# Small spaces between the buffers of the split weight panels and in front of y

## What is computed

```
# first block, per layer
h = x @ w_in                       # split into the parts of three attentions
ya = moba(a_q, a_k, a_v) * silu(a_z)      # 8 heads of 64, causal, ALiBi
yb = mla(rmsnorm(b_cq) @ w_uq, rmsnorm(b_ckv) @ w_ukv) * silu(b_z)
yc = rmsnorm(diff_attention(c_q, c_k, c_v)) * silu(c_z)
g = sigmoid(x @ w_m + b_m)
out = (ga * (ya @ w_a) + gb * (yb @ w_b) + gc * (yc @ w_c)) @ w_o
r = ALPHA * x + out
x = layernorm(r + sigmoid(r @ w_pg) * (p_i @ w_p))
# second block, per layer (modulation rows from cond @ ada_w)
h = h + gate * swiglu(modulate(rmsnorm(h)), ffn1)          # width 2816
h = h + gate * (concat(retention, stick_breaking, mamba2) @ w_out)
h = h + gate * swiglu(modulate(rmsnorm(h)), ffn2)
```

## Time and profile before

| | |
|---|---|
| median of three runs | 2030.14 us |
| runs | 2029.02, 2034.85, 2030.14 us |
| profiled execution | 2016.13 us |
| its span, first to last instruction | 2014.8 us |
| mean granted TensorE clock | 0.972 |
| TensorE busy | 1897.4 us, 94% |
| VectorE, ScalarE busy | 1311.2 us, 942.6 us |

### The profile page before, as it was taken

How to read it: one execution, slowest core, us unless ns; L and a number is a source line. 1 busy time by engine, 2 the same in 40 slices (tenths; PEclk the granted TensorE clock), 3 DMA queues, 4 the chain that set the end, 5 groups by cost and what they waited for, 6 DMA issues and landing times.

```text
span 2014.8 us, 33982 instructions
## 1 busy us (share of the span) xinstructions
PE 1897.4 (94%) x15008; PEld 1815.9 (90%) x15008; DVE 1311.2 (65%) x1850; ACT 942.6 (47%) x1266; POOL 43.8 (2%) x48
## 2 busy tenths in 40 slices
PE   7998998899899987999999889999999999999998
PEld 7987888898788886999899789999999999889998
DVE  5666677665776676666766866666666675765554
ACT  5564454445545454444455334334444455434443
POOL 0000100000010000000000000000000000000000
PEclk9999999999999998999989999999999999999999
DMA  7444356464353552766455334665566555334551
GB/s 300 178 190 157 147 204 217 163 260 178 129 223 132 208 225 118 287 251 250 168 220 200 146 127 188 251 251 230 209 244 248 199 192 209 116 120 151 197 188 63
DMA packets 59284, 389.70 MB, mean 193 GB/s; under 512 B 6656, under 2 KB 9472, under 8 KB 15232
## 3 DMA queue, kind: packets, MB, share of 16 engines
q1 hardware_dynamic: 59136, 387.52, 50.9%
HBM read 386.45 MB, written 1.05 MB: 192 GB/s over the span
## 4 chain that ended last, share of the span: by engine, by line
PE 69%; DVE 19%; ACT 10%; issue 1%; DMA 0%; POOL 0%; SPq 0%; DVEq 0%; ACTq 0%
PE bank L698 21%; PE bank L700 21%; PE bank L699 21%; DVE weights_split L847 6%; ACT weights_split L841 4%; PE bank L762 2%; ACT map L1282 1%; DVE xbc L2145 1%; DVE map_stat L1470 1%; ACT map L1288 1%; DVE weights L827 1%; PE bank L897 1%; DVE map L1464 1%; DVE hidden L2157 1%; DVE u L2163 1%
## 5 line engine op out<-in xcount | busy, mean ns | idle before, releaser
L847 DVE TENSOR_TENSOR weights_split<-weights,weights_split 128x2048 fp32r<-128x2048 f32 (+2 forms) x306 | 655.3, 2142 | 421.0 <-ACT weights_split L841 420.4
L698 PE MATMUL bank<-u,weights_split 128*128 128x256 f32 x2048 | 589.0, 288 | 17.8 <-DVE u L2163 10.1
L841 ACT CAST weights_split<-weights 128x2048 fp32r<-128x2048 f32 (+2 forms) x306 | 543.3, 1776 | 126.8 <-PE bank L700 100.8
L699 PE MATMUL bank<-u,weights_split 128*128 128x256 f32 x2048 | 577.7, 282 | 0.0
L700 PE MATMUL bank<-u,weights_split 128*128 128x256 f32 x2048 | 577.0, 282 | 0.0
L698 PEld LDWEIGHTS bank<-u,weights_split 128*128 128x128 f32 x2048 | 390.9, 191 | 25.2 <-DVE u L2163 13.4
L700 PEld LDWEIGHTS bank<-u,weights_split 128*128 128x128 f32 x2048 | 392.3, 192 | 0.0
L699 PEld LDWEIGHTS bank<-u,weights_split 128*128 128x128 f32 x2048 | 391.7, 191 | 0.5 <-issue 0.5
L698 PE MATMUL bank<-y,weights_split 128*128 128x256 f32 (+1 forms) x1168 | 331.7, 284 | 4.2 <-ACT b_k L867 4.2
L699 PE MATMUL bank<-y,weights_split 128*128 128x256 f32 (+1 forms) x1168 | 327.6, 280 | 0.0
L700 PE MATMUL bank<-y,weights_split 128*128 128x256 f32 (+1 forms) x1168 | 327.5, 280 | 0.0
(11 more groups left out here) (285 smaller groups left out, 1906.0 us busy)
## 6 DMA issues: line engine op xcount, KB each, us to landing
weights<-in_weights SPq DMA_DIRECT2D x262, 1024.0 KB, 6.5
weights<-in_ada SPq DMA_DIRECT2D x80, 1024.0 KB, 4.8
weights<-in_weights SPq DMA_DIRECT2D x36, 512.0 KB, 5.4
weights<-in_weights SPq DMA_DIRECT2D x4, 576.0 KB, 4.7
constants_second<-in_constants_second SPq DMA_DIRECT2D x1, 1792.0 KB, 12.2
weights<-in_weights SPq DMA_DIRECT2D x2, 640.0 KB, 7.6
h<-in_x SPq DMA_DIRECT2D x2, 512.0 KB, 4.9
out<-xbc SPq DMA_DIRECT2D x4, 256.0 KB, 2.2
```

Of the source, the lines that this page charges most:

```text
L698: pe.matmul(out, left[0], right[0], start=start, stop=False, **more)
L699: pe.matmul(out, left[0], right[1], start=False, stop=False, **more)
L841: act.do.copy(split[:, 0, 0:n], raw[:, 0:n]).then_inc(*self.act_wrote.inc(("weights", key)))
L847: dve.do.tensor_tensor(split[:, 1, 0:n], raw[:, 0:n], split[:, 0, 0:n].bitcast(F32), ALU.subtract).then_inc(*self.dve_wrote.inc(("weights" ...
```

## The change

Behind each of the three buffers of the split ring a tile of 32 float32 numbers (128 bytes in each partition) is allocated that nothing uses, and in front of y and of y2 one of 16 numbers (64 bytes). All that is allocated behind such a tile lies that much further back. Nothing else differs.

```diff
-        self.split = self.new_ring([self.tile(f"weights_split{i}", [P, 2, SLOT], F32R) for i in range(SPLIT_SLOTS)])
+        split = []
+        for i in range(SPLIT_SLOTS):
+            split.append(self.tile(f"weights_split{i}", [P, 2, SLOT], F32R))
+            self.tile(f"between{i}", [P, 32])
+        self.split = self.new_ring(split)
...
         b["p"] = sb("p", [P, PLE // P, 2, T], F32R)
+        sb("between_y", [P, 16])
         b["y"] = sb("y", [P, DC + 1, 2, T], F32R)
...
         b["u"] = sb("u", [P, DC, 2, T], F32R)
+        sb("between_y2", [P, 16])
         b["y"] = sb("y2", [P, HIDDEN_BLOCKS, 2, T], F32R)
```

## The result

The changed kernel takes 2013.44 us in the median (2007.42 to 2014.44, four executions), the kernel before 2030.13 (four executions). The ratio is 0.9907, with a 95% interval from 0.9882 to 0.9932: 17 us less, where 40 had been forecast. The profiled execution took 2007.42 us, its span is 2006.1 us.

What follows compares the result with a forecast made beforehand. TensorE's step per matmul was taken as the bound. 20.3 us (feed-forward) plus 12 us (rest) gave 32 us off: 1984 from the profiled execution, 1998 from the median, so 1990 us; range 1972 to 2031.

Steps and rivals of the forecast that it cites:

- the two gaits: Matmuls of `parts`: TensorE steps at about 117.8 or 113.3 ns, 4.44 ns apart, held through a stretch.
- Distances never seen: y at 0, 256 and 384: bounds 4.6 us gained below, 15.6 us lost above; taken as 0.
- the fourth rival: Slower: y's new distances turn fast streams slow or cost in every matmul; 2039, up to 2046 us; chance 0.12.
- The second rival: Part of it: only some streams turn, or y's panels interrupt the gait; half the sum, about 2010 us; chance 0.10.
- A meeting at 448 knocks: Weight and moving reads meeting in one 65,536-byte piece at distance 448 turn TensorE fast; at 64 the gait stays.
- the fallback that the prediction named: Feed-forward parts: if only buffer 2, at 192, knocks, the gain is 19.9 us in place of 20.8.
- The feed-forward term: Three slow feed-forward parts turn fast, the fourth gains nothing; 20.3 us in the sum.
- The rest: Slow matmuls outside the feed-forward parts turn fast: 10.5 to 15.4 us, middle 13, nine tenths taken, 12 us.
- the third rival: The clock takes some back: more idle in attention, more half-clock stretches; three more make it 2001 us; inside the forecast's range.
- The pair of units in the earlier trace: Between attention heads, slow-panel unit 7.98 us, fast-panel unit 7.77: 0.21 saved of 0.21, so nearly all gain arrives.
- Between the median and the profiled execution: Median 14.0 us above the profiled execution; 1,710 fast matmuls there explain 7.6 us; time put between 1984 and 1998.
- No change: First rival: gait is set by a stream's start after a break, not by distances; 2030 us; chance 0.16.

Runs made afterwards that it cites:

- the three best layouts: Kernel before with other spaces: 128 bytes behind each split buffer; 384 behind each; or 128 behind each plus 256 before y and y2: 1991.9 to 1992.1 us.
- the panels' spaces: Kernel before plus only the three 128-byte spaces behind the split buffers, none in front of y and y2: 1992.13 us, ratio 0.9815.
- The kernel with 512 bytes: Kernel before plus one 512-byte space behind the third split buffer, distances modulo 512 unchanged at 64: 2029.68 us, ratio 1.0003.
- y's spaces alone: Kernel before plus only the 64-byte spaces in front of y and y2: 2031.78 us, ratio 1.0017.
- the run with steps of 32 bytes: Kernel before plus 32-byte spaces behind each split buffer, none in front of y: 2044.93 us, ratio 1.0079.
- 192 everywhere: Kernel before plus one 128-byte space behind the third split buffer, so x, u, p and y are at 192 from all buffers: 1995.76 us, ratio 0.9860.

## Why the prediction was wrong

**The bound, and the two gaits: right.** TensorE's step decides, there are two gaits, and spaces of 32 numbers between the buffers turn the feed-forward parts fast.

**The failed step: "Distances never seen. 0, 256 and 384 with y ... I take 0."** The runs show 118.9 ns for y in the changed kernel and 113.8 without its spaces, 3504 x 5.1 ns = 18 us; measured between the two kernels, 2013.4 - 1992.1 = 21 us. Against the kernel before, y's matmuls lost only 7.4 us, inside the bound of 15.6. But the sum had already counted y's matmuls of the feed-forward parts as turned fast, and against that they cost the 18. This was the mechanism of the fourth rival, at work together with the forecast's own, and the two were treated as alternatives: the price of one was never taken off the gain of the other. The second rival, "y's panels interrupt the gait", half the sum and about 2010 us, came nearest to the measured 2013 and had a chance of 0.10. Two of the prediction's own signs of being wrong appeared: the stream turns from fast to slow at y's panels, and there is a third step above 118 ns. No row before could price this, since its full-width streams had odd multiples of 64 only and the new distances of y were the first even ones. That was visible in the listing of distances, and it was a reason to give these rivals more weight.

**The reason for taking 0 fell too.** By the split of the memory into pieces of 65,536 bytes, inferred from six slow transposed streams, reads in different pieces should not meet. But y lies in another piece than buffer 0 and steps at 120 ns with it in the changed kernel, as u does with all three buffers at distance 0.

**"A meeting at 448 knocks": wrong as a rule, right in its effect here.** At one distance, 448 or 192, nothing is knocked. What the runs show instead is that a slow stream turns fast where the weights go over from a place at 64 or 320 to one at 192 or 448: in the two `b_ckvr` panels before, and between buffers 1 and 2 in the three best layouts, at 21 of 25 such seams in slow streams. The four that did not turn are in streams of two panels. So the fallback that the prediction named (buffer 2 alone turns the stream) came nearest.

**The feed-forward term, 20.3 us: right for the panels' spaces.** Alone, they shorten the profiled execution by 24.3 us. The three parts that were slow give 20.1 of it; the fourth, fast in both, is 0.9 us longer by its first panel. In the changed kernel the same three parts give only 10, which is y's cost again.

**"The rest", 12 us: too large against the profiled execution.** With the panels' spaces alone the first matmul of u starts at 794.0 us in place of 796.6, so that the first block gained 2.6 us; the stretches between the feed-forward parts gained 2.5. That is 5 us in place of 12. In the first block the steps themselves account for more: some 3,090 matmuls are fast there in place of 1,280, 8.0 us. But stretches at a granted clock of 0.50 last 61.4 us in that block in place of 50.2, which costs up to half of the 11.2, so the clock can explain why less arrived; this is the third rival. The kernel with 512 bytes, which has the old distances, had fewer fast streams by the chance of the starts. Against it the first block gains 5.9 us and the stretches between the parts 3.6: 9.5 in all, four fifths of the term. Single panels between heads have no seam, and buffers 0 and 1 often leave them slow (x steps at 114.8 on average, not 113.3). The pair of units in the earlier trace rows was right about one unit and no measure of how many would turn.

**Between the median and the profiled execution: the right idea, with a wrong count.** The prediction has 1,710 fast matmuls before, 7.6 us. Its own rows have more: 1,560 in the fourth feed-forward part and 192 in the stream from 561.2 on the earlier trace rows. Counted again over the trace, some 3,260 matmuls step at 113.3 ns and 9,900 at 117.8. At 117.8 for all of them the execution would be 14.5 us longer, as much as the 14.0 to the median. The kernel with 512 bytes, at the old distances, has a span of 2027.0 us against 2014.8, with all four feed-forward parts slow. Of its 12.2 us more, 6.9 are the fourth feed-forward part and 3.3 the first block. From 2027.0 to the 1990.5 us of the panels' spaces alone are 36.5 us, where the forecast's sum was 32. That the forecast took 1990, between its two sums of 1984 and 1998, and the panels' spaces alone gave 1992, is in part luck: a term too large and a base too fast made up for each other.

**The rivals.** "No change" falls: 2055 and 1992 us differ in nothing but the places of the buffers. The Trainium skill, SBUF — State Buffer, "SBUF: two separate sides", states that on the engines' side only the shared port pair causes contention. What the prediction drew from that, that distances can't matter, does not agree with these two runs. Between before and after the clock took little: stretches at a granted clock of 0.50 last 122.5 us in all after and 116.2 before, 3 us of time lost.

**What stays open.** Why the seam from u to y turns a fast stream slow with 128 bytes in front of y and not with 0 or 256, although all three leave y at odd multiples of 64. At that seam both operands step, while between buffers 1 and 2 the weights alone do, and no run has a seam at which the moving operand alone steps by 128 or 256 bytes. Nor is it known what decides the gait at a start, and why 192 and 448 favour the fast one. That stationary and moving reads hinder each other in the memory is one picture for a cost that goes by their distance; no run shows the reads themselves. Of the 6 us between the 15 in the steps and the 8.7 that arrived, the clock explains up to half and the rest was not placed.

## What to carry to other kernels

Where TensorE streams matmuls with a weight load each, compute the distance between the stationary and the moving buffer and look at the step between starts, not at the printed durations. Identical stretches of code with different counts of matmuls per window are a sign of two gaits, and then the layout may decide which one a stream has; here three spaces of 32 numbers were worth 2%. In this kernel each of the four even multiples of 64 bytes modulo 512 cost in nearly every matmul, so a second space that is put in for one operand has to be checked against the first. When a change has two halves with opposite mechanisms, price both at once, and run each half alone first.

## What had not been expected of the hardware

- The step of a 128x128 by 256 matmul with its weight load is 113.3 or 117.8 ns at the full clock at distances of 64, 192, 320 or 448 bytes modulo 512. With the same instructions it is on average 120.0 at 0, 118.6 at 384, 119.8 at 256, 119.9 at 96 and about 117.5 to 118 at 160. At 128 it is 118.6 with y's spaces alone and up to 120.0 in the run with steps of 32 bytes.
- At one distance the gait holds for some 1560 matmuls in a row, through changes of buffer and operand, and is set within the first dozen after a break. A whole program varied by 24 us from one execution to the next with 192 everywhere, 1993.15 to 2017.64 us; that the gait is the reason fits, but the execution of 2017.64 us was not profiled.
- The three layouts with a seam from 320 to 192 or 448 in each long stream were not only faster but steadier than those with most streams fast at one distance: 1989.56 to 1992.45, 1990.70 to 1993.79 and 1990.77 to 1994.06 us, in four executions each.
